# Sums of a mixture of experts that start from zeros in DRAM, with x kept in SBUF

## What is computed

```
def moe_ffn(h, w_router, b_router, w_gate_up, b_gate_up, w_down, b_down):
    logits = h @ w_router + b_router
    top_v, top_i = top_k(logits, 4); top_w = softmax(top_v)
    for each expert e and each token that chose it:
        gu = h @ w_gate_up[e] + b_gate_up[e]
        glu = min(gate, 7) * sigmoid(1.702 * gate)
        out = ((clip(up, -7, 7) + 1) * glu) @ w_down[e] + b_down[e]
        y[token] += top_w * out

x = x + moe_ffn(rmsnorm(x), ...)
x = rmsnorm(x)          # the final norm of the first block
```

## Time and profile before

| | before |
|---|---|
| median of 3 runs | 2107.99 us |
| the profiled execution | 2108.63 us |
| its span, first to last instruction | 2106.9 us |
| TensorE busy | 2073.1 us (98%) |
| VectorE, ScalarE, GpSimd busy | 41%, 22%, 17% |
| granted TensorE clock, mean | 0.997 |
| moved by DMA | 520.02 MB |

### The profile page before, as it was taken

How to read it: one execution, slowest core, us unless ns; L and a number is a source line. 1 busy time by engine, 2 the same in 40 slices (tenths; PEclk the granted TensorE clock), 3 DMA queues, 4 the chain that set the end, 5 groups by cost and what they waited for, 6 DMA issues and landing times.

```text
span 2106.9 us, 42669 instructions
## 1 busy us (share of the span) xinstructions
PE 2073.1 (98%) x17798; PEld 1381.8 (66%) x17798; DVE 858.3 (41%) x1468; ACT 455.7 (22%) x741; POOL 368.7 (17%) x413
## 2 busy tenths in 40 slices
PE   9999998999999999999999999999999999999999
PEld 6888876356777777443343333347786778888887
DVE  4454535333333333333232333324575443444544
ACT  4152442000000000000000000014454533212221
POOL 2010001122222322222222222221201400000000
PEclk9999999999999999999999999999999999999999
DMA  7333114999999999999999999984121021323231
GB/s 260 100 121 130 61 40 182 414 407 404 405 406 407 405 406 408 402 408 404 400 408 400 404 405 397 408 276 144 59 81 41 1 80 61 101 98 100 80 101 58
DMA packets 157492, 520.02 MB, mean 247 GB/s; under 512 B 16460, under 2 KB 71936, under 8 KB 124576
## 3 DMA queue, kind: packets, MB, share of 16 engines
q1 hardware_dynamic: 136768, 495.02, 59.9%
q0 software_dynamic: 20672, 24.26, 4.8%
HBM read 509.09 MB, written 18.88 MB: 251 GB/s over the span
## 4 chain that ended last, share of the span: by engine, by line
PE 59%; DMA 16%; SPq 5%; ACT 1%; issue 1%; DVE 1%; POOL 0%; POOLq 0%; DVEq 0%; ACTq 0%
PE ps L2229 17%; DMA ring_a<-in_w_down 12%; PE ps L2243 11%; PE ps L396 8%; PE ps L398 8%; PE ps L397 8%; DMA ring_a<-in_w_gate_up 4%; SPq L577 3%; SPq L575 2%; PE ps L2037 1%; PE ps L2031 1%; PE ps L2094 1%; PE ps L2057 1%; PE ps L1987 1%; PE ps L2124 1%
## 5 line engine op out<-in xcount | busy, mean ns | idle before, releaser
L2229 PE MATMUL ps<-ring_a,xe 128*32 128x512 f32 x3912 | 441.6, 593 | 5.1 <-DMA ring_a<-in_w_gate_up 3.5
L2243 PE MATMUL ps<-ring_a,act_t 128*32 128x256 f32 x6000 | 339.8, 380 | 6.7 <-DMA ring_a<-in_w_down 4.5
L2229 PEld LDWEIGHTS ps<-ring_a,xe 128*32 128x32 f32 x3912 | 176.3, 110 | 240.6 <-issue 141.1
L2243 PEld LDWEIGHTS ps<-ring_a,act_t 128*32 128x32 f32 x6000 | 245.4, 110 | 106.5 <-DMA ring_a<-in_w_down 23.5
L2229 PE MATMUL ps<-ring_b,xe 128*32 128x512 f32 x2232 | 249.3, 592 | 0.0
L396 PE MATMUL ps<-xt_hi,hi 128*128 128x512 f32 x544 | 214.1, 394 | 0.8 <-DVE ff_a L1717 0.8
L397 PE MATMUL ps<-xt_lo,hi 128*128 128x512 f32 x544 | 212.1, 390 | 0.0
L398 PE MATMUL ps<-xt_hi,lo 128*128 128x512 f32 x544 | 212.0, 390 | 0.0
L2229 PEld LDWEIGHTS ps<-ring_b,xe 128*32 128x32 f32 x2232 | 101.6, 110 | 118.4 <-issue 82.6
L1124 ACT ACTIVATE glu<-glu 128x768 f32<-128x768 f32 x32 | 27.0, 844 | 658.6 <-DVE glu L1670 638.6
L774 POOL DMA_INDIRECT x_rows<-ye,idx x96 | 152.7, 1590 | 37.9 <-issue 37.9
(11 more groups left out here) (343 smaller groups left out, 2605.0 us busy)
## 6 DMA issues: line engine op xcount, KB each, us to landing
ring_a<-in_w_gate_up SPq DMA_DIRECT2D x163, 1024.0 KB
ring_a<-in_w_down SPq DMA_DIRECT2D x125, 1024.0 KB
ring_b<-in_w_gate_up SPq DMA_DIRECT2D x93, 1024.0 KB
raw<-in_w_in SPq DMA_DIRECT2D x20, 1024.0 KB, 5.9
raw<-in_w_gate SPq DMA_DIRECT2D x11, 1024.0 KB, 5.4
raw<-in_w_up SPq DMA_DIRECT2D x11, 1024.0 KB, 5.3
raw<-in_w_down SPq DMA_DIRECT2D x11, 1024.0 KB, 4.9
raw<-in_w_out SPq DMA_DIRECT2D x8, 1024.0 KB, 5.1
```

The costliest lines, as they stand in the source:

```text
L2229: last = pe.matmul(ps[QUAD * j:QUAD * j + QUAD, g, :], xe[:, g, QUAD * k:QUAD * k + QUAD], w[:, j, :, :, :], start=k == 0, stop=k == KT - 1)
L2243: last = pe.matmul(y_block(g, j, bank), act_t[:, g, QUAD * (2 * c + h):QUAD * (2 * c + h) + QUAD], w[:, h, QF * j:QF * j + QF], start=c == ...
```

## The change

- The stores of x to `x_rows` between the stages go, and with them GpSimd's wait for them. x stays in SBUF through the expert stage; the ring does not use its place.
- GpSimd sets a tile `y_zero` (128 x 1024) to zero ahead of its loads at L656. SyncE stores it four times to `x_rows`, behind the loads of chunks 2, 3, 4 and 5 of stage A. VectorE waits for the four stores before it writes `psn`, which has the same place.
- `b_dn` and `wT` become four copies, one in each quarter of the partitions. `b_dn` is loaded four times. VectorE copies `w_full` four times into `w_rep`, and the four transposes are 128 wide.
- In the first expert TensorE makes the eight products `wT` x `b_dn` (32 rows, 128 x 512 results) in groups of three, three and two after gate-up chunks 4, 5 and 6, on successive quarters of the partitions and on the banks 3, 4 and 5. VectorE adds each to x in SBUF, between its index work for the second expert and that expert's transpose. A product waits for the addition that frees its bank.
- TensorE's wait for `wT` in SBUF is before the first group, and there are waits for `b_dn`. The three `keep_warm` products write bank 6, and a wait for the eight additions follows.
- At the end SyncE loads the sums from `x_rows` into `y_back0` and `y_back1` in place of x. The first products into the eight banks are identity times x, the second identity times these sums.

```diff
-        wT = at("wT", K(52), [NE, SEQ])
-        b_dn = at("b_dn", K(54), [NE, D])
+        wT = at("wT", K(52), [P, SEQ])
+        b_dn = at("b_dn", K(54), [P, D])
+        w_rep = at("w_rep", K(33), [P, T, 4, NE])
+        y_zero = at("y_zero", K(24), [P, D])
+        y_back = [at("y_back0", 40 * KB, [P, 2, D]), at("y_back1", K(12), [P, 2, D])]
...
             for c in range(1, SA.n):
                 load_chunk(sp, SA, c)
+                if A_C <= c < A_C + T:
+                    sp.wait_ge(pads_set, 4)
+                    sp.dma_start(x_tile_rows(c - A_C), y_zero[:, :]).then_inc(y_set, 16)
...
-            for t in range(T):
-                evacuated(sp, SA, SA.first[A_END - 1] + t)
-                sp.dma_start(x_tile_rows(t), x[:, t, :]).then_inc(x_set, 16)
             sp.wait_ge(SA.lo_ready, SA.n)
             moe_loads(sp)
 
             for t in range(T):
-                sp.dma_start(x[:, t, :], x_tile_rows(t)).then_inc(row_tile[t], 16)
+                sp.dma_start(y_tile(t), x_tile_rows(t)).then_inc(row_tile[t], 16)
...
+        def y_tile(t):
+            return y_back[t // 2][:, t % 2, :]
...
             norm_rstd(pool, NS["mix"], T, EPS_1)
+            pool.memset(y_zero[:, :], 0.0).then_inc(pads_set, 1)
             pool.dma_start(scal[:, :], A["scal"]).then_inc(rows_in, 16)
...
-            pool.dma_start(b_dn[:, :], A["b_down"][0]).then_inc(m_scat, 16)
+            for j in range(4):
+                pool.dma_start(b_dn[NE * j:NE * j + NE, :], A["b_down"][0]).then_inc(bdn_in if j else m_scat, 16)
...
-            pool.wait_ge(x_set, 16 * T)
+            pool.wait_ge(y_set, 16 * T)
             gather(pool, 0, 0)
...
-            act.activation(wT[:, :], ps[0:NE, 5, :], ACT.Copy).then_inc(r_wt_sb, 1)
+            act.activation(wT[:, :], ps[:, 5, :], ACT.Copy).then_inc(r_wt_sb, 1)
...
                 if c == A_DFT:
+                    dve.wait_ge(y_set, 16 * T)
                     dve.memset(psn[:, :, 0:HALF + 1:HALF], 0.0)
...
-                link(i) if k < TOPK - 1 else i.then_inc(r_mask, 1)
+                link(i)
+            dve.tensor_copy(w_rep[:, :, :, :], w_full[:, :, :].unsqueeze(2).to_broadcast([P, T, 4, NE])).then_inc(r_mask, 1)
             dve.wait_ge(r_mask, 3)
...
             indices(1, None, 48)
             pick_row(1, 1)
+            for n in range(2 * T):
+                dve.wait_ge(r_wt, 2 + n)
+                xs = x[:, n // 2, 512 * (n % 2):512 * (n % 2) + 512]
+                dve.tensor_tensor(xs, ps[:, 3 + n % 3, :], xs, ALU.add).then_inc(x_biased, 1)
             x_transpose(1, 8)
...
                 for n in range(2):
-                    mm(bd_banks(t)[:, n, :], wT[:, t * P:(t + 1) * P], b_dn[:, 512 * n:512 * n + 512], start=True, stop=False,
+                    mm(bd_banks(t)[:, n, :], ident, x[:, t, 512 * n:512 * n + 512], start=True, stop=False,
                        skip_group_check=True)
             for t in range(T):
                 pe.wait_ge(row_tile[t], 48)
                 for n in range(2):
-                    last = mm(bd_banks(t)[:, n, :], ident, x[:, t, 512 * n:512 * n + 512], start=False, stop=True,
+                    last = mm(bd_banks(t)[:, n, :], ident, y_tile(t)[:, 512 * n:512 * n + 512], start=False, stop=True,
                               skip_group_check=True)
...
+            def down_bias(n):
+                if n >= 3:
+                    pe.wait_ge(x_biased, n - 2)
+                q, t, o = NE * (n % 4), n // 2, 512 * (n % 2)
+                pe.matmul(ps[:, 3 + n % 3, :], wT[q:q + NE, t * P:(t + 1) * P], b_dn[q:q + NE, o:o + 512],
+                          start=True, stop=True, skip_group_check=True).then_inc(r_wt, 1)
...
                     for t in range(T):
-                        last = pe.transpose(ps[0:NE, 5, t * P:(t + 1) * P], w_full[:, t, :], ident)
+                        last = pe.transpose(ps[:, 5, t * P:(t + 1) * P], w_rep[:, t, :, :].rearrange("p q e -> p (q e)"), ident)
                     last.then_inc(r_wt, 1)
-            pe.wait_ge(r_wt_sb, 1)
-            keep_warm(pe, 5, 3)
+                if j == 4:
+                    pe.wait_ge(r_wt_sb, 1)
+                    pe.wait_ge(m_scat, 16)
+                    pe.wait_ge(bdn_in, 48)
+                if j >= 4:
+                    for n in range(3 * (j - 4), min(3 * (j - 3), 2 * T)):
+                        down_bias(n)
+            keep_warm(pe, 6, 3)
+            pe.wait_ge(x_biased, 2 * T)
             with pe.Fori(0, n1) as i:
```

More of the change, by code:

```diff
@@ L324, in program @@
             ("inputs", "weights_split", "logits_done", "shifted", "exp", "masks", "positions",
-             "weightsT", "weightsT_sb"))
+             "weightsT_and_bias_products", "weightsT_sb"))
         r_lgT, r_lgT_sb = sem("route_logitsT"), sem("route_logitsT_sb")
@@ L336, in program @@
         m_y, m_scat, xg_zero, held = (sem(s) for s in ("m_y", "m_scattered", "xg_zero", "m_held"))
-        x_set = sem("x_rows_set")
+        y_set = sem("y_rows_set")
+        bdn_in, x_biased = sem("down_bias_loaded"), sem("x_biased")
         bd_done, f_ss, f_rstd, f_x = (sem(f"final_{s}") for s in
```

## The result

The changed kernel takes 2111.49 us (median of 20 runs, 2105.45 to 2113.25) against 2107.68 us (20 runs, 2104.0 to 2109.41) of the kernel before, measured side by side: a ratio of 1.0016, with a 95% interval of 1.001 to 1.0023. By the ratio that is 3.4 us more, inside the 0.2% that the forecast takes for no change. The interval excludes 1, though, so the changed kernel is a little slower, and its upper end lies above 0.2%. The profiled execution took 2112.68 us.

What follows compares the result with a forecast made beforehand. The prediction took the DMA engines to bound the expert stage. Copy and products, 0.4 + 3.7 = 4.1 us, against 2.2 us to spare at ring load 20 gave +1.8 us: 2109.8 us, own range 2107 to 2112.5.

Steps and rivals of the forecast that it cites:

- What bounds the kernel: Expert stage: the DMA engines are full, share 1.01 to 1.03, so it ends with the end of its bytes.
- The stores of x give at most what there is to spare at chunk 20: Ring load 20, second expert: removing 5.1 us of stores gains 2.2 us, the spare before the DMA engines run dry.
- the milder form of the first rival: Some DMA idle time is made up by a better rate over the following 970 us; 0.5% would be 5 us.
- w_rep: VectorE's fourfold copy of the weights ahead of the first expert: 0.48 us, starting that expert 0.37 us later.
- The eight products, 3.7 us: Down-bias products on TensorE in the first expert: groups of 1.3, 1.3 and 1.06 us; bounds 1.8 to 7.6 us.
- The additions cost nothing: VectorE's eight additions in the first expert, 5.5 us in all, fit its idle 15.06 us: no cost.
- Nothing, with 3 us to spare: Early stage: memset and zeros delay constants, splits end about 37 us, TensorE wants the chunk at 39.98 us: no cost.
- The end: Behind the last scatter: sums are loaded as x was, with as many product instructions as before: no cost.
- rival of bytes in full: Expert stage: the ring was never the limit, so the removed 5.1 us of transfers all count: 2102.9 us; chance 0.18.
- that of a free lead: Expert stage: TensorE's lead of 470 us hides the products' 4 us; no chance of its own given.
- that of serial products: First expert: the products don't overlap, TensorE spends 8.0 us with the copy, +5.7 us, 2113.7 us; chance 0.23.
- The marks: Signs named beforehand: first expert about 379.2 us, groups 1.1 to 1.3 us, chunk 20 issued 410.4 us, DMA share below 1.

Runs made afterwards that it cites:

- e7: The kernel before, with x stored a second time into memory nobody reads, right behind the first stores: 2113.37 us, ratio 1.0036 to the kernel before.
- e4: The kernel before, with eight idle 128x512 products nobody reads behind gate-up chunk 6 of the first expert: 2113.55 us, ratio 1.0028 to the kernel before.
- e2: The changed kernel with GpSimd's memset behind its loads and the four stores of zeros two chunks later: 2109.73 us, ratio 1.0013 to the kernel before.
- e1: The changed kernel without its eight products and eight additions, so the down bias is left out: 2106.81 us, ratio 0.9992 to the kernel before.
- e8: The changed kernel with late zeros, serial products and additions in block 17, transposes ahead of the first expert: 2105.8 us, ratio 0.9996 to the kernel before.
- e3: The kernel before with late zeros and without the stores of x, x left out of the sums, no new products: 2105.16 us, ratio 0.999.
- e6: The changed kernel with the four stores of x put back, into memory nobody reads: 2111.24 us, ratio 1.002 to the kernel before.
- e5: The changed kernel with all eight products on the first quarter of the partitions: 2114.69 us, ratio 1.0041 to the kernel before.
- e9: e8 with two of the thirteen filling products ahead of the first expert taken out: 2104.27 us, ratio 0.9984 to the kernel before.

## Why the prediction was right, and where it was not

**What bounds the kernel: right.** The stage behaves as "the end of its bytes" as long as loads can be issued, and as TensorE's time up to chunk 20 plus a constant when they can't. In the nine kernels where chunk 20 is late enough or x is not stored, its issue and the end of the stage are 971.8 to 972.9 us apart, while its issue itself moves by over 10 us against the first store of h.

**The stores of x give at most what there is to spare at chunk 20: right in kind, a little smaller.** Forecast 2.2 us. What a kernel has against the one before at the end of the stage, beyond what it has at chunk 20, is the last column of distances in the table: 973.78 less its value, so 1.0 us in the changed kernel and 0.9 to 2.0 us in the nine kernels (all but before and e7), 1.3 in the mean. With the stores of x in place it is the spare alone (e4: 2.0 us of 6.9 were hidden). *This is one mis-sized term.* The loss is made at chunk 20 and not over the long stretch behind it. 150 us behind the first store of h, SyncE's queue had moved 55.79 MB in the kernel before, 53.60 in e4 and 52.26 in the changed kernel. Less 2.10 MB for x in the first two, and at the 0.388 MB per us that this queue moves over the rest of the stage, that is 5.6 us behind in e4 and 3.7 us behind in the changed kernel. Of the 6.90 and 4.97 us at chunk 20, 1.3 us are hidden in both; the nine kernels have 1.1 to 1.8 us there, 1.5 in the mean. So the milder form of the first rival, idle time made up by a better rate afterwards, isn't needed, and the 1 us by which e4 and the changed kernel differ at the end of the stage arose later; its cause stays open. The working set 1.91 MB and a load's time on idle queues against each other, and both ends can carry an error of some tenths; which of the two was off isn't settled by these runs.

**w_rep: right.** The copy takes 0.43 us (forecast 0.48). In e2 the first expert starts 39.68 us behind the first store of h and waits for the turned rows, where it was 39.43: +0.25 us against +0.37. In the changed kernel itself it could not be seen, since TensorE was the later one there, as the next rows show. VectorE and TensorE after:

```profile
374.26 0.43 DVE L1607 COPY w_rep<-w_full 128x512 f32<-128x512 f32 x1
...
379.97 0.97 DVE L1674 STREAM_TRANSPOSE xe<-xg 128x768 f32<-128x768 f32 x1
```

```profile
368.91 13.12 PE L2139 MATMUL ps<-const 128*128 128x512 f32 x26 [1.58 <-DVE n_blk L1583]
...
382.19 5.32 PE L2244 MATMUL ps<-ring_a,xe 128*32 128x512 f32 x48
```

**The eight products, 3.7 us: right in sum, not in its parts.** The groups took 1.06, 1.07 and 1.06 us, 3.2 us in all; the forecast allowed 1.3 for a group of three. The missing 0.4 us lies in the gate-up chunks around them: from start to start of the rows, chunks 3 to 7 without the products' groups take 13.42 us, and 13.01 us in e1, where nothing interrupts them. That is 0.14 us for each of three interruptions. It need not be the price of another tiling of the array. In e4 one interruption by full products of 128 rows costs the same (20.22 us from the start of chunk 3 to the next filling products, less 7.06 for the eight products and 13.02 for the chunks in the kernel before). And the four transposes of the kernel before, whose form is 128*32 like that of the gate-up products, cost 0.16 us beyond their own 0.54, by the chunks around them in e8, where they are elsewhere (16.25 and 15.55 us from chunk 2 to the end). The estimate by the Trainium skill (TensorE: Matmul & The Clock Gate, Measured speedup vs the span model), a factor of 3.07 for four products, is supported in kind by the factor of 2.6 for three; no run here has four. TensorEngine Tiling (Key Properties) of the Trainium skill says that a change of tiling mode drains the engine; no run here shows such a drain by itself, and what an interruption costs, 0.14 us, is small.

**The additions cost nothing: right.** VectorE after, with no wait of TensorE for it:

```profile
397.12 1.89 DVE L1708 TENSOR_TENSOR x<-ps,x 128x512 f32<-128x512 f32 x3 [8.32 <-PE ps L2267]
```

The first three ended at 399.01 us, before the next group began at 399.73. In e8, where VectorE's additions stood behind other work, TensorE did wait (2.65 us): the cover was needed.

**"Nothing, with 3 us to spare" in the early stage: wrong.** *This is the step that failed*, and one of the signs that the prediction named for being wrong, the stage before 340 us moving, did appear: the stage is 0.8 us longer. The forecast was that the constants come up to 3.8 us later by the shared DMA engines and 1 us by the memset. GpSimd's timeline after, and the chain of waits:

```profile
21.08 0.95 POOL L663 MEMSET y_zero<- 128x1024 f32 x1
```

```profile
23.15 11.45 DMA const<-in_const
```

The memset was as priced. But the constants took 11.45 us from their issue; before they had been issued at 21.02 us and were awaited until 27.58, 6.6 us. That is 4.9 us more, not 3.8. And the work that the delay reached first was not the chunk that TensorE wants at 39.98 us. VectorE and TensorE after:

```profile
36.64 4.50 DVE L387 TENSOR_TENSOR lo<-raw,hi 128x2048 fp32r<-128x2048 f32 x2 [7.99 <-ACT hi L380]
41.05 2.48 DVE L1249 TENSOR_TENSOR u_lo<-ps,u_hi 128x512 fp32r<-128x512 f32 x4
```

```profile
41.88 0.47 PE L400 MATMUL ps<-xt_hi,hi 128*128 128x512 f32 x1 [0.56 <-DVE u_lo L1249]
```

Behind the late splits on VectorE's queue stand four remainders `u_lo`, which before began at 34.01 us. They went last, and TensorE waited 0.56 us for them. The prediction asked when the delayed work is wanted, and not what is queued behind it on the same engine. 0.56 us of the 0.80 is this wait; the other 0.2 us isn't assigned.

**The end: right.** From the last row of expert products to the next norm's first product it takes 44.1 us, and 44.2 before.

**The sum.** With the measured terms: 0.8 (early stage) + 0.25 (copy) + 3.6 (products) - 1.3 (spare) = +3.35 us; the ratio says 3.4, with an interval of 2.1 to 4.8, so that the sum fits it but is not proved by it to a tenth. The dip of the clock ahead of the first expert, some 1.1 us in the profiled execution, is not in this sum. The forecast had 0 + 0.4 + 3.7 - 2.2 = +1.9 (+1.8 in its own rounding), so 2109.8 us. The measured 2111.49 us is inside the forecast's own range of 2107 to 2112.5, and the terms it had wrong, the early stage and the spare, both err to the same side: the hit is not two errors that cancel. The forecast's rival of bytes in full is refuted by e3 and e6, that of a free lead by e1 and e4, and that of serial products by the groups of 1.06 us, with e5 to show what they would have cost.

**The marks.** As named: the DMA share below 1 between 400 and 420 us, groups of about 1.1 us, full engines behind them. Not as named: the first long wait for weights was to come at about the time it had, 869.16 us, but came at 847.77. Why isn't shown: a later TensorE alone doesn't do it, since in e4, where it is later still, the first such wait comes at 963.40. Chunk 20 was issued 2.9 us later than the 410.45 forecast: 1.23 us by the start of the span, 0.8 by the early stage, and 0.9 mostly by the clock, below. For the same reasons the first expert began at 382.19 us and not at about 379.2.

## What to carry to other kernels

Where a ring of buffers feeds full transfer queues, bytes removed ahead of it are worth only the distance between the moment at which the queues would run dry and the moment at which the next load is released; compute that distance before trading TensorE's time for bytes. Put new work where the engine waits for data and not where its pace releases loads, and far enough from the end that it can catch up: the same eight products, even slower ones, were free 17 blocks later, but it took TensorE some 330 us to catch up. And when a step is delayed, look at what stands behind it on its engine's queue, not only at who wants its result.

## What was not expected of the hardware

**TensorE's clock drops to half for some us, at places that differ between kernels with the same instructions there.** It differs between executions of one kernel too: the mean clock of the changed kernel's 20 runs lies between 0.996 and 0.999. In the changed kernel the 13 filling products ahead of the first expert took 13.12 us, in the kernel before 11.42 us with the same rows ahead of them: eight small products and a wait of 1.6 us. Between 368.9 and 372.0 us the clock granted to the changed kernel is 0.60, so for most of that stretch it is at the lower of its two levels, 1.2 in place of 2.4 GHz. Stretches of the changed kernel, then of the kernel before (columns as in the earlier trace rows):

```profile
355.00:381.90 26.90, 22.59 (x78) 10.74 (x78) 20.14 (x100) 0.70 (x4) 4.48 (x5) 0.94 1.02 404
...
1500.00:1525.00 25.00, 22.93 (x121) 17.84 (x119) 13.02 (x19) 11.83 (x22) 9.60 (x2) 1.00 0.18 59
```

```profile
1500.00:1525.00 25.00, 22.56 (x115) 16.82 (x114) 12.37 (x19) 12.95 (x29) 3.94 (x1) 0.93 0.13 42
```

The clock granted is below full in one kernel at 369 us and in the other at 1511 us, in the attention of the second block. Of the eleven profiled executions five show a clock of 0.96 between 340 and 382 us (after, e1, e5, e6 and e9), six don't. The first four are just the kernels with early zeros, so whether the change makes this dip more likely stays open; if it does, the early zeros cost more than the 0.8 us above, by the 1.1 us that e2 has less than the changed kernel between the first store of h and chunk 20. A dip ahead of chunk 20 costs the stage (e1 started its first expert at 40.6 us behind the first store of h, e2, with the same copy ahead of it, at 39.7), and a dip in the second block costs there: of the 2.0 us which the changed kernel gains behind the stage the greater part is the dip that it does not have there (0.07 x 25 us = 1.75 us by the two granted clocks). From the end of the last long wait to the end of the span the kernel before, e1 and e9 take 726.8 to 727.3 us, and the eight others 724.6 to 725.3, e3, e4 and e7 among them, which have nothing of the change there. So the 2.0 us are not the change's. In e9 a second dip falls into block 17, between 919 and 930 us, with a clock of 0.53, following a wait of 2.79 us and products of 32 rows, and does not show at the end of the stage.

**Products of 32 rows in three quarters of the array ran entirely beside each other**: 1.06 us for two as for three, 1.91 and 2.77 us in one quarter.
